# Hybrid decoder step: the prompt tiles' output projection, norm, modulation and routers move between the sample batches

## The chip, the cores and the metric

One core of a Trainium2 chip runs the kernel. Its engines work side by side, each through its own program in order: TensorE (PE, matrix products and transposes), VectorE (DVE), ScalarE (ACT), GpSimd (POOL) and SyncE (SP, which here only sends for transfers). Semaphores tie them together. The metric is the device time of one execution in microseconds; less is better.

## The reference, cut to what matters

One layer is computed for two groups of tokens with the same weights: a prompt of 256 tokens (two tiles of 128 rows), and 8 samples of 8 new tokens (one tile of 64 rows), each sample with a cache of 2048 keys and values. All is float32, D = 1024.

```
shift1, scale1, gate1, shift2, scale2, gate2 = split(silu(c) @ w_ada + b_ada)   # per sequence
u   = x * (1 + scale1) + shift1
q, k, v, B, C, h = split(u @ w_in)
mix = concat(rms(attention(q, k, v, cache)), rms(B * conv3(C * h))) @ w_o
x   = LN1(alpha * x + (1 + gate1) * mix)
u2  = x * (1 + scale2) + shift2
x   = LN2(alpha * x + (1 + gate2) * MoE(u2))    # router, top 4 of 32 experts, clamped SwiGLU
```

gate1, shift2 and scale2 are one vector of 1024 for the prompt and one for each of the 8 samples. The outputs are both groups' x, the new keys, values and convolution rows.

## The kernel before, in words

The stages follow one another on PE, whose program is written out by hand; the other engines' programs mirror it.

1. *Start*: w_ada and w_in stream through a ring of six buffers; PE computes the modulation vectors (kept as 32-row groups in `ada_sb`, bias added), and all projections of all 320 tokens (`q_t`, `k_t`, `v_nat`).
2. *Prompt attention*, head by head, and the turning of the first sample's keys. Then the table of position biases (`s_bias`), and the norm of the prompt's attention output: `squares(0)`, `sums_of_squares(0)`, `mean_squares(0)`, a root on ACT, then `inverse_roots(0)` and `scale(0)`, which run on DVE in batch 7.
3. *Sample batches*, one for each of 8 samples (`pe_batch`, `dve_batch`, `act_batch`; batches 1 to 6 are a hardware loop). PE: scores against 1280 cached keys and the 64 new ones (line 1368), `heads_apart` of the batch before (L1376), transposes of the next batch's keys (`keys(0)`, `keys(1)`, through `turn`, L1155), transposes of the probabilities (L1155), `keys(2)`, product with V (L1417). ACT and DVE copy the turned keys out of PSUM in turns (L558, L819); DVE adds the bias and takes the maximum (L936 to L941), ACT the exponential (L601); DVE takes the reciprocal (L956) and makes the masked output (L961). K and V have one buffer each: SP sends for the next K once the keys are turned, and for the next V when the product with V has used it.
4. *The stage behind the batches*. PE: `output(0)`, `sums_of_squares(1)`, `output(1)` (L1445), `output(2)` (L1438), and three routers (transposes of u2, L1155; 8 products with the router's weights, L1462; the bias, L1463). DVE, in an order written out: residual(0), residual(1), route(0), residual(2), route(1), route(2). `residual` is the gated residual, the layer norm (`layer_norm`, L1720 to L1727) and the modulation (L1002, L1003); `route` (L1010 to L1024) picks four experts and makes the gates. gate1, scale2 and shift2 come as rows of 128 or 64 partitions: POOL wrote them to DRAM during the prompt's attention, and SP reads them back with a broadcast (`mod_p`, `mod_s`). Then the ranks of tokens in each expert (L1480, L1484) and the first gather (L1495).
5. *Experts*: a loop over 32 experts (the data asks for no second round), in which PE uses each expert's 12 MB of weights as they land, then the last norm.

PSUM has 8 banks of 512 columns. In a batch the scores lie in banks 0 to 2, turned keys in 3 to 6, turned probabilities in 5 to 7, the product with V in 7.

## Time and profile before

| | |
|---|---|
| median of 3 runs | 1557.39 us (1557.28 to 1561.96) |
| the profiled execution's own time | 1561.42 us |
| its span, first to last instruction | 1559.6 us |
| mean granted clock of PE | 0.962 of full speed |
| busy: PE, DVE, ACT | 1439.7, 496.6, 244.1 us |
| read from DRAM | 519.87 MB, 336 GB/s over the span |

The span is 2 us short of the same execution's time, and that execution was 4 us longer than the median. Times of single instructions come from this one execution. PE's busy time is that of its products with modelled ends; every float32 product shows as two records. The granted clock is given as a share of 2.4 GHz: 0.50 is the lower of two levels, 1.2 GHz. A wait is written behind an instruction as [idle before it <- what ended the idle time]; "issue" means that the profile shows nothing that was waited for.

### The profile page before, as it was taken

What the parts mean: (1) busy time and instruction counts of PE and PEld (TensorE: products, weight loads), DVE (VectorE), ACT (ScalarE), POOL (GpSimd) and SP (SyncE); (2) the same over time, 40 slices, a digit from 0 to 9 for tenths busy, and PEclk for the clock granted to TensorE, in tenths of its full rate; (3) what the DMA queues carried; (4) which work ended last, traced back from release to release, by engine and by line L of the source; (5) the groups of instructions that cost most, each with busy time, mean ns of one, the idle gap of its engine ahead of it and who ended that gap; (6) DMA issues with size and microseconds to landing.
All of it is one profiled execution on the core that took longest, in us unless ns stands there. A gap on an engine that the chain in (4) does not pass through costs nothing.

```text
span 1559.6 us, 22176 instructions
## 1 busy us (share of the span) xinstructions
PE 1439.7 (92%) x7709; PEld 595.4 (38%) x7710; DVE 496.6 (32%) x1129; ACT 244.1 (16%) x431; POOL 12.0 (1%) x20
## 2 busy tenths in 40 slices
PE   5999998898967999999999999999999999999993
PEld 1654655655442333333333333333333333333331
DVE  2111354444382222322232212232232232222236
ACT  0001423332020111111111101111111111111110
POOL 0000000000010000000000000000000000000000
PEclk9999999999877999999999999999999999999997
DMA  9958268996663679999999988999999999988940
GB/s 341 364 209 319 103 254 315 365 347 261 206 257 128 252 324 387 410 416 417 418 417 415 418 341 324 380 417 417 418 417 416 418 418 416 417 348 317 387 203 34
DMA packets 95700, 523.72 MB, mean 336 GB/s; under 512 B 10156, under 2 KB 10469, under 8 KB 55482
## 3 DMA queue, kind: packets, MB, share of 16 engines
q1 hardware_dynamic: 92496, 517.62, 83.5%
q0 software_dynamic: 1344, 4.90, 0.8%
q10 hardware_dynamic: 1834, 0.84, 0.2%
q8 instruction: 17, 0.28, 0.1%
q14 instruction: 9, 0.07, 0.0%
HBM read 519.87 MB, written 3.46 MB: 336 GB/s over the span
## 4 chain that ended last, share of the span: by engine, by line
PE 86%; DVE 5%; issue 3%; DMA 2%; ACT 2%; SPq 0%; DVEq 0%; ACTq 0%
PE ps L1573 29%; PE ps L1649 15%; PE ps L1517 7%; PE ps L1155 7%; PE ps L1495 5%; PE ps L1215 5%; PE ps L1417 3%; PE ps L1368 2%; PE ps L1565 2%; PE ps L1212 2%; PE ps L1445 2%; DMA arena<-in_w_ada 2%; PE ps L1583 1%; PE ps L1190 1%; ACT arena L672 1%
## 5 line engine op out<-in xcount | busy, mean ns | idle before, releaser
L1573 PE MATMUL ps<-arena 128*64 128x512 f32 x2048 | 460.1, 607 | 0.5 <-issue 0.5
L1573 PEld LDWEIGHTS ps<-arena 128*64 128x64 f32 x2048 | 146.4, 139 | 312.5 <-issue 312.5
L1649 PE MATMUL ps<-arena 128*64 128x512 f32 x1024 | 228.5, 599 | 20.5 <-ACT arena L672 15.1
L1155 PE MATMUL ps<-arena 128*128 128x128 f32 (+4 forms) x1075 | 153.7, 283 | 46.5 <-DVE arena L819 12.5
L1058 DVE TENSOR_TENSOR arena<-arena,ps 128x512 f32<-128x512 f32 (+1 forms) x198 | 123.9, 680 | 203.4 <-PE ps L1517 197.9
L1155 PEld LDWEIGHTS ps<-arena 128*128 128x128 f32 (+4 forms) x1075 | 116.7, 144 | 120.8 <-issue 77.2
L1102 DVE TENSOR_SCALAR arena<-ps 128x512 f32<-128x512 f32 (+1 forms) x35 | 24.2, 692 | 426.7 <-PE ps L1573 360.5
L1649 PEld LDWEIGHTS ps<-arena 128*64 128x64 f32 x1024 | 73.5, 137 | 155.0 <-issue 155.0
L1517 PE MATMUL ps<-arena 64*128 64x512 f32 x444 | 114.6, 622 | 2.2 <-ACT arena L655 2.0
L1495 PE MATMUL ps<-arena 128*64 128x512 f32 (+1 forms) x396 | 98.5, 613 | 2.6 <-DVE arena L1046 2.6
L666 ACT ACTIVATE arena<-arena 128x512 f32<-128x512 f32 (+1 forms) x35 | 22.1, 632 | 456.8 <-DVE arena L1102 456.8
L1215 PE MATMUL ps<-arena 128*128 128x320 f32 x288 | 83.9, 444 | 3.1 <-DVE arena L749 3.1
L1517 PEld LDWEIGHTS ps<-arena 64*128 64x128 f32 x444 | 36.6, 185 | 76.6 <-issue 59.7
L1215 PEld LDWEIGHTS ps<-arena 128*128 128x128 f32 x288 | 54.9, 195 | 28.4 <-issue 5.6
L1082 DVE COPY arena<-ps 128x512 f32<-128x512 f32 (+1 forms) x37 | 24.2, 664 | 108.9 <-PE ps L1155 108.9
L704 ACT COPY arena<-ps 128x512 f32<-128x512 f32 x29 | 17.0, 587 | 258.4 <-PE ps L1517 258.4
L1495 PEld LDWEIGHTS ps<-arena 128*64 128x64 f32 (+1 forms) x396 | 25.5, 137 | 69.3 <-issue 69.3
L666 ACT ACT_TABLE_LOAD x32 | 41.1, 1283 | 38.0 <-issue 38.0
L558 ACT COPY arena<-ps 128x512 f32<-128x512 f32 (+1 forms) x63 | 32.3, 513 | 91.5 <-PE ps L1155 91.5
L1417 PE MATMUL ps<-arena 128*32 128x256 f32 (+1 forms) x528 | 42.7, 395 | 2.2 <-DMA arena<-in_cache_v 2.2
L1368 PE MATMUL ps<-arena 128*32 128x512 f32 (+2 forms) x384 | 39.5, 462 | 2.2 <-DVE arena L923 2.2
L819 DVE COPY arena<-ps 128x512 f32<-128x512 f32 (+1 forms) x63 | 37.2, 599 | 12.8 <-PE ps L1155 11.8
(225 smaller groups left out, 862.0 us busy)
## 6 DMA issues: line engine op xcount, KB each, us to landing
arena<-in_w_up SPq DMA_DIRECT2D x256, 1024.0 KB, 12.8
arena<-in_w_down SPq DMA_DIRECT2D x128, 1024.0 KB, 10.8
arena<-in_w_ada SPq DMA_DIRECT2D x12, 2048.0 KB, 17.5
arena<-in_cache_k SPq DMA_DIRECT2D x16, 1536.0 KB, 8.7
arena<-in_cache_v SPq DMA_DIRECT2D x16, 1536.0 KB, 9.0
arena<-in_w_in SPq DMA_DIRECT2D x6, 2048.0 KB, 20.4
arena<-in_cache_k SPq DMA_DIRECT2D x32, 192.0 KB, 4.1
arena<-in_cache_v SPq DMA_DIRECT2D x32, 192.0 KB, 9.6
```

The source lines that it names most:

```text
L558: nc.scalar.copy(kt_sb[:, c, 512 * kt:512 * kt + w], bank(key_bank(kt * AC + c), 0, w)).then_inc(kt_act, 1)
L666: nc.scalar.activation(act_s[0:p, v, :], act_g[0:p, v, :], ACT.Sigmoid, scale=1.702).then_inc(sig_ready[v], 1)
L819: v_.tensor_copy(kt_sb[:, c, 512 * kt:512 * kt + w], bank(key_bank(kt * AC + c), 0, w)).then_inc(kt_dve, 1)
L1058: ins = v_.tensor_tensor(acc[0:n, tt, 512 * h:512 * h + 512], acc[0:n, tt, 512 * h:512 * h + 512], bank(banks[h])[0:n], ALU.add)
L1155: return nc.tensor.transpose(o, i, ident[0:n, 0:n])
L1215: ins = mm(bank(unit_bank(u))[:, 0:NTOK], w[:, k, col:col + 128], u_t[:, k, :], start=k == 0, stop=k == KC - 1)
L1368: ins = mm(o[32 * j:32 * j + 32], qbd[:, c, :], rhs(c), start=c % 2 == 0, stop=c % 2 == 1, tile_position=(0, 32 * j))
L1417: ins = mm(bank(7, 0, 256)[32 * g:32 * g + 32], pt_sb[0:n, j, 32 * g:32 * g + 32], rhs, start=j == 0, stop=j == KB, tile_position=(0, 32 * g))
L1495: ins = mm(bank(4)[64 * h:64 * h + 64], sel[0:n, tt, 0:MAIN], u2[0:n, tt, 512 * h:512 * h + 512], start=tt == 0, stop=tt == 2)
L1517: ins = mm(bank(banks[h]), sel_t[64 * h:64 * h + 64, v, 128 * tt:128 * tt + 128], y_sb[64 * h:64 * h + 64, v, :], start=v == 0, stop=v == ...
L1573: ins = mm(bank(part)[64 * h:64 * h + 64], xe_t[:, 0, at:at + 64], up_w[:, k, FF * part + 512 * h:FF * part + 512 * h + 512], start=False, ...
L1649: ins = mm(bank(3)[64 * h:64 * h + 64], a_t[:, 0, at:at + 64], dn_w[:, kk, 512 * h:512 * h + 512], start=kk == 0, stop=kk == KC - 1)
```

## The change

- Memory: the batches' buffers (`s_bias`, `prob`, `pt_sb`, `qbd`, `o_mask`) move from R1 and R2 into R4, over the prompt's q, k and v, which are now kept apart from the samples' (`q_p`, `q_s`, `k_p`, `k_s`, `v_p`, `v_s`). R1 and R2 are then free during the batches for `x1` and `u2`.
- x and the gains and offsets of LN1 are loaded by POOL's queue during the batches, not by SP's behind them. The write of the modulation vectors to DRAM and their broadcast back are gone.
- The rows of gate1, scale2 and shift2 are made by PE: a product of a matrix of zeros and ones (`rep_p`, `rep_s`) with the 32-row group of `ada_sb`, two products of 512 columns for a vector.
- `inverse_roots(0)` and `scale(0)` run in batch 0. `output(0)` and `output(1)` run in batches 1 and 2, into banks 0 and 1, from which ACT copies them to `u2`. The prompt's modulation products run in batches 3, 5 and 6; DVE does the residual and the statistics of both tiles in batch 3, the norm in 4, the scale in 5 and the shift in 6. ACT takes the norm's roots in batch 4. In batch 7 PE makes the samples' three vectors (ACT copies them to `mod_s`) and runs the routers of tiles 0 and 1.
- Behind the batches only the samples' norm, `output(2)`, residual(2), router(2) and route(2) are left in front of the ranks.
- The loop over the batches is written out on all three engines.

```diff
-        mod_p = view(W + 18 * D, 3, D)
-        mod_s = view(W + 21 * D, 3, D)
+        mod_s = view(W + 18 * D, 3, D)
...
+        v_s = view(R4, DA)
+        v_p = view(R4 + 768, 2, DA)
+        v_tile = [v_p[:, 0], v_p[:, 1], v_s]
+        q_p = view(R4 + 2304, AC, SEQ)
+        q_s = view(R4 + 3840, AC, 64)
+        k_p = view(R4 + 4224, AC, SEQ)
+        k_s = view(R4 + 5760, AC, 64)
+
+        s_bias = view(R4 + 768, SB)
+        prob = view(R4 + 768 + SB, NCACHE + 64)
+        pt_sb = view(R4 + 4224, KB + 1, 96)
+        qbd = view(R4 + 4224 + (KB + 1) * 96, AC, 32)
+        o_mask = view(R4 + 4224 + (KB + 1) * 96 + AC * 32, 256)
...
-            sp.wait_ge(so_copied, NB)
-            sp.dma_start(x1[:, 0:2, :], t["x_prompt"][0].rearrange("(a p) d -> p a d", p=128)).then_inc(tail_in, 16)
-            for a, name in enumerate(("ln1_g", "ln1_b")):
-                sp.dma_start(ln1[:, a, :], t[name][0:1, :].to_broadcast([128, D])).then_inc(tail_in, 16)
-            sp.wait_ge(vec_out, 64)
-            sp.dma_start(mod_p, vectors[0:1, 0:3 * D].to_broadcast([128, 3 * D]).rearrange("p (a b) -> p a b", a=3)
-                         ).then_inc(mod_in, 16)
-            for b in range(NB):
-                src = vectors[1 + b:2 + b, 0:3 * D].to_broadcast([NS, 3 * D]).rearrange("p (a b) -> p a b", a=3)
-                sp.dma_start(mod_s[NS * b:NS * b + NS], src).then_inc(mod_late, 16)
-            sp.dma_start(x1[0:64, 2, :], t["x_sample"].rearrange("b s d -> (b s) d")).then_inc(mod_late, 16)
...
-            pool.wait_ge(ada_late, 1)
-            for j in range(4):
-                pool.dma_start(vectors.rearrange("r (m j c) -> j r m c", m=2, j=4)[j],
-                               ada_sb[32 * j:32 * j + 1 + NB, 1:3, :]).then_inc(vec_out, 16)
             pool.wait_ge(out_kv, 96)
+            pool.wait_ge(sb_done, 1)
+            pool.dma_start(x1[:, 0:2, :], t["x_prompt"][0].rearrange("(a p) d -> p a d", p=128)).then_inc(tail_in, 16)
+            pool.dma_start(x1[0:64, 2, :], t["x_sample"].rearrange("b s d -> (b s) d")).then_inc(tail_in, 16)
+            pool.dma_start(ln1[1], t["ln1_b"][0:1, :].to_broadcast([128, D])).then_inc(tail_in, 16)
+            pool.wait_ge(og_ready, 1)
+            pool.dma_start(ln1[0], t["ln1_g"][0:1, :].to_broadcast([128, D])).then_inc(tail_in, 16)
...
-                    ins = nc.scalar.mul(q_t[:, c, :], src[:, 0:NTOK], HD ** -0.5)
+                    nc.scalar.mul(q_p[:, c, :], src[:, 0:SEQ], HD ** -0.5)
+                    ins = nc.scalar.mul(q_s[:, c, :], src[:, SEQ:NTOK], HD ** -0.5)
...
+            def act_mix(tt):
+                act.wait_ge(wo_done, tt + 1)
+                for h in range(2):
+                    ins = nc.scalar.copy(u2[:, tt, 512 * h:512 * h + 512], bank(h))
+                ins.then_inc(mix_ready, 1)
+
+            def act_keep_mods(a):
+                act.wait_ge(mods_done, a + 1)
+                for h in range(2):
+                    ins = nc.scalar.copy(mod_s[0:64, a, 512 * h:512 * h + 512], bank(3 + h)[0:64])
+                ins.then_inc(mods_kept, 1)
...
+                if b == 4:
+                    act.wait_ge(var_ready, 2)
+                    nc.scalar.activation(st[:, 66:68], st[:, 64:66], ACT.Sqrt).then_inc(sd_ready, 1)
...
+                if b in (1, 2):
+                    act_mix(b - 1)
...
+            for b in range(NB):
+                act_batch(b)
+            for a in range(3):
+                act_keep_mods(a)
+            act_turn(0)
+            act_exp(0)
+            act_turn(1)
+            act_exp(1)
...
+            def prompt_residual():
+
+                dve.wait_ge(mod_done, 1)
+                for tt in range(2):
+                    V(v_.scalar_tensor_tensor(u2[:, tt, :], ps[:, 0:D], 1.0, u2[:, tt, :], ALU.add, ALU.mult))
+                dve.sem_inc(mod_used, 1)
+                dve.wait_ge(tail_in, 64)
+                for tt in range(2):
+                    V(v_.scalar_tensor_tensor(x1[:, tt, :], x1[:, tt, :], ALPHA, u2[:, tt, :], ALU.mult, ALU.add))
                     for h in range(2):
-                        ins = v_.scalar_tensor_tensor(m[:, 512 * h:512 * h + 512], mod[0:n, 0, 512 * h:512 * h + 512], 1.0,
-                                                      bank(4)[64 * h:64 * h + 64], ALU.add, ALU.mult)
+                        ins = v_.bn_stats(st[:, 48 + 6 * h:54 + 6 * h], x1[:, tt, 512 * h:512 * h + 512])
                     V(ins)
-                dve.wait_ge(tail_in, 48)
-                x_t = x1[0:n, tt, :]
-                V(v_.scalar_tensor_tensor(x_t, x_t, ALPHA, m, ALU.mult, ALU.add))
-                layer_norm(dve, V, v_, x_t, n, st, ln1, var_ready, sd_ready, tt + 3, x_t)
-                V(v_.scalar_tensor_tensor(u2[0:n, tt, :], mod[0:n, 2, :], 1.0, x_t, ALU.add, ALU.mult))
-                V(v_.tensor_tensor(u2[0:n, tt, :], u2[0:n, tt, :], mod[0:n, 1, :], ALU.add))
-                dve.sem_inc(u2_ready, 1)
+                    V(v_.bn_aggr(st[:, 60 + 10 * tt:62 + 10 * tt], st[:, 48:60]))
+                    V(v_.tensor_scalar(st[:, 64 + tt:65 + tt], st[:, 61 + 10 * tt:62 + 10 * tt], LN_EPS, None, ALU.add))
+                dve.sem_inc(var_ready, 1)
+
+            def prompt_normal():
+
+                dve.wait_ge(sd_ready, 2)
+                V(v_.reciprocal(st[:, 66:68], st[:, 66:68]))
+                for tt in range(2):
+                    x_t = x1[:, tt, :]
+                    V(v_.scalar_tensor_tensor(x_t, x_t, st[:, 60 + 10 * tt:61 + 10 * tt], ln1[0], ALU.subtract, ALU.mult))
+                    V(v_.scalar_tensor_tensor(x_t, x_t, st[:, 66 + tt:67 + tt], ln1[1], ALU.mult, ALU.add))
+
+            def prompt_scaled():
+
+                dve.wait_ge(mod_done, 2)
+                for tt in range(2):
+                    V(v_.scalar_tensor_tensor(u2[:, tt, :], ps[:, 0:D], 1.0, x1[:, tt, :], ALU.add, ALU.mult))
+                dve.sem_inc(mod_used, 1)
+
+            def prompt_shifted():
+
+                dve.wait_ge(mod_done, 3)
+                for tt in range(2):
+                    V(v_.tensor_tensor(u2[:, tt, :], u2[:, tt, :], ps[:, 0:D], ALU.add))
+                    dve.sem_inc(u2_ready, 1)
+                dve.sem_inc(mod_used, 1)
...
+                if b == 0:
+                    inverse_roots(0)
+                    scale(0)
+                if b == 3:
+                    prompt_residual()
+                if b == 4:
+                    prompt_normal()
+                if b == 5:
+                    prompt_scaled()
+                if b == 6:
+                    prompt_shifted()
+                if b == 7:
+                    route(0)
+                    route(1)
...
+            residual(2)
+            route(2)
...
+            GATE1, SHIFT2, SCALE2 = (1, 0), (1, 2), (2, 0)
+
+            def modulation(which, n, lhs, b, done):
+
+                m, j = which
+                for h in range(2):
+                    at = 32 * (j + h)
+                    ins = mm(bank(b + h)[0:n], lhs[at:at + 32, 0:n], ada_sb[at:at + 32, m, :], start=True, stop=True)
+                ins.then_inc(done, 1)
+
+            def beside_batch(b):
+                if b == 1:
+                    pe.wait_ge(og_ready, 1)
+                    pe.wait_ge(wo_in, 16)
+                if b in (1, 2):
+                    output(b - 1)
+                if b in (3, 5, 6):
+                    if b == 3:
+                        pe.wait_ge(ada_late, 1)
+                    modulation({3: GATE1, 5: SCALE2, 6: SHIFT2}[b], 128, rep_p, 0, mod_done)
+                if b == 7:
+                    for a, which in enumerate((GATE1, SCALE2, SHIFT2)):
+                        if a:
+                            pe.wait_ge(mods_kept, a)
+                        modulation(which, 64, rep_s, 3, mods_done)
+                    router(0)
+                    router(1)
+
+            def banks_free(b):
+
+                if b in (2, 3):
+                    pe.wait_ge(mix_ready, b - 1)
+                if b in (4, 6, 7):
+                    pe.wait_ge(mod_used, {4: 1, 6: 2, 7: 3}[b])
...
+                if more:
+                    beside_batch(b)
...
+                if not more:
+                    beside_batch(b)
+                pe.wait_ge(v_in, b * 96 + 96)
...
+            for b in range(NB):
+                pe_batch(b)
+            heads_apart(NB - 1)
+
+
+            pe.wait_ge(so_copied, NB)
             sums_of_squares(1)
-            output(1)
             pe.wait_ge(og_ready, 2)
             output(2)
-            router(0)
-            router(1)
             router(2)
```

## Rows read from the trace of the kernel before

**Rows 1.** The page's chain that ended last: shares of the span by engine.

```profile
PE 86%; DVE 5%; issue 3%; DMA 2%; ACT 2%; SPq 0%; DVEq 0%; ACTq 0%
```

**Rows 2.** Windows: stretch, its length, busy time (instructions), granted clock, DMA share, GB/s.

```profile
243.87:265.77 21.90, 19.45 (x200) 12.97 (x203) 9.50 (x24) 7.77 (x13) 0.00 (x0) 1.00 0.93 345
...
403.00:441.00 38.00, 37.92 (x112) 16.59 (x112) 17.06 (x31) 1.80 (x3) 0.00 (x0) 0.96 0.97 320
...
446.00:456.20 10.20, 6.13 (x26) 5.55 (x26) 9.48 (x27) 2.78 (x4) 0.00 (x0) 0.50 0.43 145
```

**Rows 3.** Order of time, TensorE, a middle batch: start, duration, instructions [idle before].

```profile
328.89 1.54 PE L1155 MATMUL ps<-arena 96*128 96x96 f32 x15 [0.77 <-ACT arena L558]
...
332.69 5.08 PE L1417 MATMUL ps<-arena 128*32 128x256 f32 x66
```

**Rows 4.** Order of time, DVE and ACT, the same middle batch and the next scores.

```profile
323.39 1.42 ACT L601 ACTIVATE arena<-arena 96x1344 f32<-96x1344 f32 x1
...
333.03 0.16 DVE L956 RECIPROCAL arena<-arena 96x1 f32<-96x1 f32 x1
...
342.61 0.22 DVE L936 SCALAR_TENSOR_TENSOR arena<-ps,arena 96x64 f32<-96x64 f32 x1 [4.24 <-PE ps L1368]
```

**Rows 5.** Order of time, batch 7, all engines and SP's transfers of V.

```profile
381.06 0.81 SPq L372 DMA_DIRECT2D arena<-in_cache_v  x2
...
382.09 3.34 DVE L872 RECIPROCAL arena<-arena 128x512 f32<-128x512 f32 x1
...
390.16 2.00 PE L1155 MATMUL ps<-arena 96*128 96x96 f32 x11 [2.50 <-ACT arena L601]
...
392.60 0.24 DVE L952 COPY arena<-ps 64x96 f32<-64x96 f32 x1
...
392.95 2.47 DVE L877 SCALAR_TENSOR_TENSOR arena<-arena 128x256 f32<-128x256 f32 x6
...
394.32 6.35 PE L1417 MATMUL ps<-arena 128*32 128x256 f32 x66 [2.17 <-DMA arena<-in_cache_v]
```

**Rows 6.** Order of time, TensorE, from batch 7 to the first expert.

```profile
403.08 15.70 PE L1445 MATMUL ps<-arena 128*128 128x512 f32 x32 [0.30 <-DVE arena L929]
...
420.34 13.95 PE L1445 MATMUL ps<-arena 128*128 128x512 f32 x32
434.23 7.09 PE L1438 MATMUL ps<-arena 128*64 128x512 f32 x32
...
449.38 1.94 PE L1155 MATMUL ps<-arena 128*128 128x128 f32 x8 [3.63 <-DVE arena L1012]
...
455.55 0.63 PE L1463 MATMUL ps<-arena 1*128 1x32 f32 x2
...
470.00 2.41 PE L1480 MATMUL ps<-arena 128*128 128x32 f32 x12 [3.41 <-DVEq L1028]
...
489.13 1.13 PE L1565 MATMUL ps<-arena 1*64 1x512 f32 x4 [3.04 <-issue]
```

**Rows 7.** Order of time, DVE and ACT, the same stretch.

```profile
420.98 1.28 ACT L594 ACT_TABLE_LOAD   x1 [29.19 <-DVE arena L867]
...
425.18 1.22 DVE L990 SCALAR_TENSOR_TENSOR arena<-arena,ps 128x1024 f32<-128x1024 f32 x1
...
429.26 0.15 DVE L1723 TENSOR_SCALAR arena<-arena 128x1 f32<-128x1 f32 x1
...
451.94 1.39 DVE L995 SCALAR_TENSOR_TENSOR arena<-arena,ps 64x512 f32<-64x512 f32 x2
...
460.65 1.22 DVE L1003 TENSOR_TENSOR arena<-arena 64x1024 f32<-64x1024 f32 x1
...
466.69 0.18 DVE L1010 COPY arena<-ps 64x32 f32<-64x32 f32 x1 [1.39 <-PE ps L1463]
```

**Rows 8.** The product of line 1527: duration ns min/median/max, first and last start, forms.

```profile
L1527 PE MATMUL ps<-arena x12: 585/587/692, 1526.4 to 1533.7; 32*128 32x512 f32 x8, 32*64 32x512 f32 x4
```

More of the change, by code:

```diff
@@ new lines, in _, with residual @@
+            queries(slice(0, NS))
+            for b in range(NB):
+                dve_batch(b)
+            keep_output(NB - 1)
+            dve.wait_ge(so_copied, NB)
+            dve.wait_ge(po_copied, AC)
+            dve.wait_ge(out_kv, 96)
+            squares(1)
+            mean_squares(1)
+            inverse_roots(1)
+            scale(1)
+            def residual(tt):
+                n = TILES[tt][1]
+                m = mix[0:n]
+                dve.wait_ge(mods_kept, 3)
+                dve.wait_ge(wo_done, tt + 1)
+                for h in range(2):
+                    ins = v_.scalar_tensor_tensor(m[:, 512 * h:512 * h + 512], mod_s[0:n, 0, 512 * h:512 * h + 512], 1.0,
+                                                  bank(4)[64 * h:64 * h + 64], ALU.add, ALU.mult)
+                V(ins)
+                x_t = x1[0:n, tt, :]
+                V(v_.scalar_tensor_tensor(x_t, x_t, ALPHA, m, ALU.mult, ALU.add))
+                layer_norm(dve, V, v_, x_t, n, st, ln1, var_ready, sd_ready, tt + 2, x_t)
+                V(v_.scalar_tensor_tensor(u2[0:n, tt, :], mod_s[0:n, 1, :], 1.0, x_t, ALU.add, ALU.mult))
+                V(v_.tensor_tensor(u2[0:n, tt, :], u2[0:n, tt, :], mod_s[0:n, 2, :], ALU.add))
+                dve.sem_inc(u2_ready, 1)
@@ L1449, in router @@
             def router(tt):
-                n = TILES[tt][1]
+                n, first = TILES[tt][1], 0 if tt < 2 else 6
                 pe.wait_ge(u2_ready, tt + 1)
@@ L1461, in router @@
                 for k in range(KC):
[L1462 to L1467 removed]
+                    mm(bank(first, 0, NE)[0:n], u2_t[tt][:, k, 0:n], rw_sb[:, k, :], start=k == 0, stop=False)
+                mm(bank(first, 0, NE)[0:n], ones[0:1, 0:n], rb_sb[0:1, :], start=False, stop=True).then_inc(lg_done, 1)
```

283 lines of the change are left out of this document (122 added, 161 removed).

## The prediction

> **What bounds the kernel now.** I read the page's chain first. TensorE has 86% of it, DVE 5%, DMA 2% [rows 1]: this is a kernel in which the order on one engine sets the time, and a microsecond put on that engine is lost unless it fills a hole there. Then I read the table of windows [rows 2]. A middle sample batch takes 21.90 us, of which PE is busy 19.45; the DMA engines are busy 93% of it too, so either could be the pace. The order of time of a batch decides it [rows 3]: PE's holes are three or four of 0.3 to 0.8 us, each ended by a copy out of PSUM on DVE or ACT (0.77 before the transposes of the probabilities), and V's product starts with no wait for a transfer. In eight batches one transfer is waited for, V of batch 7, for 2.17 us [rows 5]. So batches are paced by PE and have about 2.4 us of holes each, made of short hand-overs that stay where they are.
>
> Behind the batches lies the stage that the change takes apart. From the end of V's product in batch 7 (394.32 + 6.35 = 400.7) to the first expert's bias product at 489.13 [rows 5, 6] there are 88.5 us. Its first half is the three output products, PE busy 37.92 of 38.00 us [rows 2]; behind them DVE works already on tile 0. Its second half, from 441 on, is a chain of short steps through DVE, ACT and PE at a granted clock of 0.50 [rows 2, 6, 7]. The experts behind it are the same program in both versions, and start later or earlier as a whole. So the account has two columns: what each batch grows by, and what is left of the 88.5 us.
>
> **The change, part by part.** *Output products of tiles 0 and 1*, 16 products of 512 columns each, go between batches 1 and 2, in front of the transposes and behind the waits for exp and the key copies, so they fill none of the holes. They took 15.70 and 13.95 us in the stage [rows 6]; the first began at a lower clock. In the batches the clock is 1.00 [rows 2], so 13.95 each: **+27.9**. Their results are copied by ACT (two of 512 columns) ahead of its last key copies; those wait in part anyway: 0 to 1.2 us a batch, I take **+0.5** in all.
>
> *Modulation rows by products.* Two products each with 32 rows contracted. The same form stands at the end of the kernel: 4 records of 585 ns, that overlap [rows 8], at 0.43 start to start 1.7 us per vector. Three vectors for the prompt, in batches 3, 5 and 6: **+5.2**. In exchange the writes to DRAM and the broadcast reads go; they lay on queues under the output products and nobody waited for them: 0.
>
> *Work on DVE in the batches.* It is put behind the reciprocal of a batch and ahead of the masked output. Between these the engine has, from 333.03 to the next scores at 342.61, 9.6 us, less 0.5 for the masked output itself [rows 4]. Batch 0 gets the inverse roots and the scaling: 3.34 + 2.47 and two more of the same form, 0.9, is 6.7 us [rows 5]. Batch 3 gets the residual and the statistics of two tiles: one tile took 425.18 to 429.41, 4.2 us [rows 7], two 8.5. Batch 4 gets 5.3 us, 5 and 6 get 2.5 each (steps of 1.2 to 1.3 us). All fit under V's product and the next scores, batch 3 with 0.6 us to spare: 0. With that cover gone, the next scores' maximum would be late by as much, and PE behind it.
>
> *A square root among the exponentials.* ACT's table changes in front of batch 0's exp, and in batches 4 and 5. A load is 1.28 us [rows 7]. Behind the exp of a batch (1.42 us) stand the key copies that free PE's banks [rows 4], so in batch 4 load and root, 1.5 us, come through; batch 5's load stands between a copy and the exp, 1.3; batch 0's 0.7. From nothing to 4: **+3.5**. The Trainium skill (ScalarE: Activation LUTs, "What ACT_TABLE_LOAD costs" and "Table sets") speaks against this edit: each switch is 1.283 us of load and about 1.38 of drain, and all calls of one set should be made before the next. The load agrees with the row; no drain shows in the transition's record, where the root starts as the load ends. By the page's sum three switches would cost 4.1 us more.
>
> *Batch 7.* Once PE has turned the probabilities and they are copied (392.60 + 0.24, [rows 5]) it does, in front of V's product, the sample's three modulation vectors, each waiting for two ACT copies of the one before, and then two routers, the second waiting for DVE's maximum of the first. V came in at 394.3, so only 1.3 us of this lies in a hole. A router at the half clock ran from 449.38 to 456.2, 6.8 us; 6.2 of them are PE's own, so at full clock some 4 to 4.5 [rows 6]. The vectors: three of 1.7 and two gaps of 1.4 are 7.9 us, at half clock 13.0. With 0.75 between the routers the block is 17.5 us at full clock and 27.3 at half. PE had been at half clock when it came here (its transposes took 2.00 us for 11 records, against 1.54 for 15 in a middle batch [rows 3, 5]), and the stretch of the second router in the trace stayed at 0.50 throughout, with PE busy 6.13 of 10.20 us [rows 2]. So I take it near the half-clock end: 25.3, less the 1.3: **+24** (bounds 16 and 26).
>
> *What is left of the stage*, counted from the end of V's product: masked output, heads apart, copy, as before, 2.4 (403.08 less 400.7); squares 0.9 (estimate, by columns from the 1.22 us of 1024); sums of squares 1.6 (between the two output products); mean to scaled, 420.34 to 425.2, 4.9; output of tile 2 7.09, and 1.75 for a clock that fell in this gap, as at 403; residual of tile 2, 451.94 to 461.9, 10.0; router 462.9 to 466.7, 3.9; routing 466.69 to 470.00, 3.3; from there to 489.13 unchanged, 19.1 [rows 6, 7]. Sum 55.1 against 88.5: **-33.4** (bounds -35 without the clock, -28 if tile 2's whole product ran at half). Note what goes: 29.65 of it is the two products, which are paid again in the batches; the rest of the old chain is shorter by about 11, but the norm of the sample tokens, which hid under tile 1's product, lies bare now, 7.4 us.
>
> *Free or nearly so.* The first expert's weights wait, as before, for the last use of V; 8 MB at the 3.93 MB in 13 us that V takes [rows 5] are 27 us, and 55 us hold them. The q and k copies split in two lie under projections of 4 us. Inputs x and the norm's vectors come early by another queue, 2.25 MB, in batches 0 and 1, which have got longer.
>
> Sum: 27.9 + 0.5 + 5.2 + 3.5 + 24 - 33.4 = **+27.7 us**. The profiled execution's own time was 1561.4 (span 1559.6), so 1589 for one like it. The median of the runs shown is 4.0 below it: **1585 us**.
>
> **Rivals.** *1. The transfers pace the batches.* If DMA at 93% were the limit, the 33 us of inserted PE work would vanish in it, and -33.4 + 24 + 4 leaves 1552: faster. It tips the sign if more than 27.7 of the 33.1 is hidden. For it: the share. Against: no batch but the last waits for a transfer; V is sent for at 381.06 and is there at 394.3, 13 us, where a middle batch has 16.8 from one use to the next (21.90 less 5.1, [rows 2, 3]). 0.05. *2. The clock stays high in batch 7*, and the table switches hide: 16 in place of 24 and 1 for 3.5, 1574. 0.15. *3. DVE is the new wait*: its 8.5 us in batch 3, or the seven pieces with their semaphores, overrun, 1 to 2 us in four batches, and tile 2's product runs at half clock: some +8, 1593. 0.13. *4. The chain is sped up by less waiting than I count* (hand-overs of PSUM while PE is on output products close holes of 2.4 us in six batches and the routers overlap): at most -14 from holes, 1571; it would need the full clock too to come near 1557. 0.03, with a third of it no change. The forecast itself 0.64, its own range 1577 to 1592.
>
> **How the numbers follow.** All low bounds together give 27.9 + 0 + 5.2 + 0.7 + 16.2 - 35.1 = +15, 1572; all high ones 27.9 + 2.4 + 5.2 + 4.1 + 26 - 28 = +38, 1595. The range reaches a little past both: 1570 to 1596; rival 1 and what is unthought of stay outside. A measurement here tells 0.3%, 4.7 us, from no change. Faster: rival 1, 0.05. Same: 0.02. Slower: 0.93.
>
> **What would show it.** Batches 1 and 2 of about 36 us, with PE never waiting for a transfer; 3, 5, 6 about 23.6; in batch 7 some 25 us between the transposes' copies and V's product, at a granted clock near 0.5; some 55 us from there to the first expert's bias product; experts at their old period. I am wrong if batches 1 and 2 are under 30 us (then transfers were the pace), if batch 7's block is under 15, or if the last stretch is under 45.

## The result and the profile after

The changed kernel takes **1586.02 us** (median of 4 runs, 1583.29 to 1590.64) against 1557.34 of the kernel before on the same chip: ratio 1.0176 (95%: 1.015 to 1.0202). It is slower, by 28.7 us; forecast were 1585.0 and a range of 1570 to 1596. A second comparison gave 1587.77 against 1558.03, ratio 1.0202 (1.0181 to 1.0222). The profiled execution of the changed kernel took 1583.29 us, its span is 1581.1. One of the four executions of the doubled products below took 6975 us, in a slow state, and is left out there.

The page's slices and chain of the kernel after:

```profile
PE   4999989988774999999999999999999999999994
...
PEclk9999999999765999999999999999999999999997
...
PE 86%; DVE 6%; issue 3%; ACT 3%; DMA 2%; SPq 0%; DVEq 0%; ACTq 0%
```

and the same two slices of the kernel before:

```profile
PE   5999998898967999999999999999999999999993
...
PEclk9999999999877999999999999999999999999997
```

The chain is still TensorE's [rows 1]. The dip in the 11th to 13th slices (395 to 514 us in the kernel after) has become longer and deeper: PE's busy share is 7, 7 and 4 tenths where it was 9, 6 and 7, and its clock 7, 6 and 5 where it was 8, 7 and 7. Three windows of the kernel after (stretch, length, busy time and instructions of PE, its weight loads, DVE, ACT, POOL, granted clock, DMA share, GB/s): a batch with an output product in it, the new block of batch 7, and the last stretch ahead of the experts.

```profile
277.02:312.52 35.50, 33.28 (x232) 19.01 (x235) 9.46 (x24) 7.34 (x14) 0.00 (x0) 1.00 0.60 223
422.90:445.90 23.00, 18.04 (x64) 12.00 (x64) 3.28 (x21) 5.83 (x11) 0.00 (x0) 0.50 0.00 1
490.00:512.00 22.00, 14.71 (x63) 6.87 (x63) 8.63 (x50) 2.56 (x4) 0.00 (x0) 0.50 0.30 119
```

A middle batch of before was 21.90 us with 19.45 of PE [rows 2]; with the output product it is 35.50 with 33.28: 13.6 us more, for 13.8 more of PE, so next to nothing was filled. DMA's share fell from 0.93 to 0.60 and the batch is longer by the whole product, so transfers were not the pace. In batch 7 PE's clock is 0.50, with PE busy 18.04 of 23.00 us.

TensorE in order of time, kernel after, batches 1 to 6 (start, duration, instructions, idle before and what ended it):

```profile
259.37 13.97 PE L1463 MATMUL ps<-arena 128*128 128x512 f32 x32 [0.98 <-ACT arena L557]
...
276.95 5.08 PE L1561 MATMUL ps<-arena 128*32 128x256 f32 x66
...
312.45 5.08 PE L1561 MATMUL ps<-arena 128*32 128x256 f32 x66
...
330.48 1.13 PE L1490 MATMUL ps<-arena 32*128 32x512 f32 x4 [0.88 <-ACT arena L557]
331.54 1.57 PE L1223 MATMUL ps<-arena 96*128 96x96 f32 x15
...
351.75 2.40 PE L1223 MATMUL ps<-arena 128*128 128x128 f32 x20 [1.42 <-ACT arena L557]
...
376.06 2.40 PE L1223 MATMUL ps<-arena 128*128 128x128 f32 x20 [1.09 <-ACT arena L557]
```

L1463 is the output product of a prompt tile in two halves of 512 columns, L1561 the product with V, L1490 a modulation vector. The starts of V's product in batches 0 to 6 are 241.23, 276.95, 312.45, 335.36, 359.27, 384.11 and 406.90: batches of 35.7, 35.5, 22.9, 23.9, 24.8 and 22.8 us where they had been 21.9 (two of them 22.4 and 22.7 in the profiled execution). The modulation costs 1.06 us a batch (330.48 to 331.54), not 1.7. The last two lines are new waits of batches 4 and 5, behind the table loads on ACT. PE waits for no transfer between 241 and 446.

The same view from batch 7 to the first expert:

```profile
406.90 5.08 PE L1561 MATMUL ps<-arena 128*32 128x256 f32 x66
...
423.33 1.97 PE L1490 MATMUL ps<-arena 32*64 32x512 f32 x4 [0.84 <-DVE arena L1039]
426.45 1.97 PE L1490 MATMUL ps<-arena 32*64 32x512 f32 x4 [1.15 <-ACT arena L624]
429.58 1.97 PE L1490 MATMUL ps<-arena 32*64 32x512 f32 x4 [1.16 <-ACT arena L624]
431.48 1.97 PE L1223 MATMUL ps<-arena 128*128 128x128 f32 x8
...
439.17 1.94 PE L1223 MATMUL ps<-arena 128*128 128x128 f32 x8 [0.87 <-DVE arena L1004]
...
445.90 6.84 PE L1561 MATMUL ps<-arena 128*32 128x256 f32 x66
...
456.10 2.57 PE L1414 MATMUL ps<-arena 128*128 128x64 f32 x12 [1.19 <-DVE arena L886]
...
464.34 9.88 PE L1456 MATMUL ps<-arena 128*64 128x512 f32 x32 [4.81 <-DVE arena L905]
484.39 1.11 PE L1223 MATMUL ps<-arena 64*128 64x64 f32 x8 [10.17 <-DVEq L1092]
...
491.57 2.41 PE L1582 MATMUL ps<-arena 128*128 128x32 f32 x12 [3.34 <-DVEq L1096]
...
512.27 1.99 PE L1667 MATMUL ps<-arena 1*64 1x512 f32 x8 [2.38 <-issue]
```

From 423.33 to 445.90 lies the new block: 8.15 us of modulation (three vectors of 1.97, the end of each included, and two gaps) and 14.4 us of two routers. Behind V's product, which ends at 452.7, come the sums of squares (L1414), the norm (a hole of 4.81), the output product of tile 2 (L1456, 9.88 against 7.09 in [rows 6]), its residual (10.17 of PE's idle time), the last router and the routing. The first expert's bias product is at 512.27, against 489.13 [rows 6].

The account of the two profiled executions:

| stretch | before | after | difference | forecast |
|---|---|---|---|---|
| to V's product of batch 0 | 243.79 | 241.23 | -2.6 | +0.7 |
| V's product of batch 0 to that of batch 6 | 132.70 | 165.67 | +33.0 | +36.4 |
| V's product of batch 6 to that of batch 7 | 17.83 | 39.00 | +21.2 | +24 |
| from there to the first expert's bias | 94.8 | 66.4 | -28.4 | -33.4 |
| to the first expert | 489.13 | 512.27 | **+23.1** | **+27.7** |

Of the first difference 1.7 us are not the change's: batch 0's scores took 6.42 us at a lower clock in the execution before and 4.72 in this one, and in the second profile of the changed kernel they took 6.42 again. The sum is 4.6 us short of the forecast, and the medians are nevertheless 28.7 and 29.7 apart.

One part of what is missing lies in the experts, which I had taken as unchanged. From one expert's bias product to the next, an ordinary expert takes 29.86 us before and 30.08 after, in all of the 22 ordinary gaps: 22 x 0.22 = 4.8 us. Two more gaps went from 33.13 to 33.33. The other seven, the first and six around experts with two blocks, differ from execution to execution (38.4 to 42.1 the first; 44.2 or 45.9 and 32.5 or 34.1 the six), and in the profiled pair they fell to the advantage of the changed kernel by 7 us: the experts' whole stage (first to last bias product) took 1005.0 us before and 1003.0 after. That is why the spans differ by 21.5 us only. A second profile of each kernel gives the same picture: first bias 489.51 and 513.57, periods 29.86 and 30.08, stage 1005.3 and 1003.1. Both profiles of the kernel before were 4 us above its median and both of the changed kernel 3 us below its own. That 23.1 + 4.8 = 27.9 is near the medians' distance is thus a reckoning which takes the seven gaps as equal in the long run; no profile shows a pair that far apart.

### The profile page after: what moved, and what is told of

The parts are those of the page before. It is cut to its first block, busy times and chain, and to the rows that moved or that the text cites. A ratio compares the mean times of both kernels' runs of the same rounds, so it can differ in the third digit from the quotient of the medians.

```text
span 1581.1 us, 21918 instructions
## 1 busy us (share of the span) xinstructions
PE 1446.4 (91%) x7733; PEld 627.1 (40%) x7734; DVE 496.5 (31%) x1134; ACT 241.3 (15%) x440; POOL 12.1 (1%) x20
## 4 chain that ended last, share of the span: by engine, by line
PE 86%; DVE 6%; issue 3%; ACT 3%; DMA 2%; SPq 0%; DVEq 0%; ACTq 0%
PE ps L1675 28%; PE ps L1751 14%; PE ps L1619 7%; PE ps L1223 7%; PE ps L1597 5%; PE ps L1283 5%; PE ps L1561 2%; PE ps L1667 2%; DMA arena<-in_w_in 2%; PE ps L1437 2%; PE ps L1280 2%; PE ps L1463 2%; PE ps L1685 1%; ACT arena L696 1%; PE ps L1258 1%
## 5 line engine op out<-in xcount | busy, mean ns | idle before, releaser
L1675 PE MATMUL ps<-arena 128*64 128x512 f32 x2048 | 453.0, 599 | 0.0
L1675 PEld LDWEIGHTS ps<-arena 128*64 128x64 f32 x2048 | 148.8, 138 | 302.6 <-issue 302.5
L1751 PE MATMUL ps<-arena 128*64 128x512 f32 x1024 | 228.3, 597 | 26.6 <-ACT arena L696 20.5
L1751 PEld LDWEIGHTS ps<-arena 128*64 128x64 f32 x1024 | 97.0, 137 | 137.4 <-issue 135.0
L1561 PE MATMUL ps<-arena 128*32 128x256 f32 (+1 forms) x528 | 43.1, 398 | 0.0
L1667 PE MATMUL ps<-arena 1*64 1x512 f32 x256 | 35.7, 627 | 4.9 <-issue 4.5
```

The costliest lines, as they stand in the source:

```text
L1561: ins = mm(bank(7, 0, 256)[32 * g:32 * g + 32], pt_sb[0:n, j, 32 * g:32 * g + 32], rhs, start=j == 0, stop=j == KB, tile_position=(0, 32 * g))
L1667: ins = mm(bank(part)[64 * h:64 * h + 64], ones[64 * part:64 * part + 1, 0:64], row, start=True, stop=False)
L1675: ins = mm(bank(part)[64 * h:64 * h + 64], xe_t[:, 0, at:at + 64], up_w[:, k, FF * part + 512 * h:FF * part + 512 * h + 512], start=False, ...
L1751: ins = mm(bank(3)[64 * h:64 * h + 64], a_t[:, 0, at:at + 64], dn_w[:, kk, 512 * h:512 * h + 512], start=kk == 0, stop=kk == KC - 1)
```

## The experiments

All were compared with the kernel before on the same chip (its medians: 1558.03 for the first four, 1559.01 for the next two, 1559.09 for the three paddings, 1558.88 for the last two). "First bias" is the start of the first expert's bias product in the profile.

### What the two kernels scatter by

The kernels before and after, unchanged, with more runs.

> The kernel before, once more with a profile, since the one profiled execution was 4 us above the median of its kernel and that of the changed kernel 3 us below its own. Theory A (the difference lies between 225 and 490 us: 23 us in the two profiles, and the rest is which execution was profiled): the time to the first expert's bias product is again 489 us within 2, the experts' period 29.87, and the execution's scatter of 4 us lies in the experts' stage or in the first transfers. Rival B (the experts' period is itself a property of each program): the period is 29.87 in every execution of this kernel and 30.08 in every one of the changed kernel.

> The changed kernel once more with a profile. Theory A: first bias product at 512 us within 2, ratio of the medians 1.015 to 1.018, and the experts' period is 29.87 or 30.08 by chance of the execution. Rival B: the period is 30.08 again, some 0.21 us for each of 25 ordinary experts, 5 us of the difference, which my sum does not have at all and which comes from something in the program other than the moved work.

Measured: before 1558.24 (10 runs), ratio 1.0002 (0.9987 to 1.0018), first bias 489.51; after 1587.77, ratio 1.0202, first bias 513.57. The ratio of the changed kernel was expected at 1.015 to 1.018 and came out above; the two comparisons of it lie 0.3% apart. The period is 29.86 in both profiles of the kernel before and 30.08 in both of the changed one, so it belongs to the program and not to an execution.

### Are the output products hidden in the batches?

The products of batches 1 and 2 are made twice, into the same banks; the work is the reference's, done twice.

```
                 if b in (1, 2):
+                    output(b - 1, False)    # no semaphore at its end
                     output(b - 1)
```

> The products of output(0) and output(1) in batches 1 and 2 are made twice over; nothing else changes. Theory A (batches are paced by TensorE, and what is put in adds its whole length): batches 1 and 2 grow from 35.7 to 49.6 us each and the kernel by 27.9 us. Rival (transfers set the pace, products in the batches are partly hidden): they grow by less than 10 each, and the kernel by under 20.

Measured: 1603.52 (the three executions of 1602 to 1607 us), ratio 1.0306 (1.0282 to 1.0329), first bias 538.34. TensorE in order of time:

```profile
262.73 27.70 PE L1463 MATMUL ps<-arena 128*128 128x512 f32 x64 [0.98 <-ACT arena L557]
...
311.96 27.70 PE L1463 MATMUL ps<-arena 128*128 128x512 f32 x64 [0.77 <-ACT arena L557]
```

The two batches take 49.4 and 49.2 us, 13.7 longer each: a microsecond put here is a microsecond lost, up to twice the amount that the change put in, and the wait ahead of the product is the same 0.98 and 0.77. This ends rival 1. But the kernel became slower by 16 to 17 us only, not by 27.9; by the kernel's time alone the rival ("under 20") would have won, and it is the length of the two batches that decides. The first bias came 24.8 to 26.1 us later, and the experts behind it were faster: 997.2 us from first to last bias product for 1003.0, with a period of 29.87 us. This miss made me follow the experts' period, below.

### The square root among the exponentials

ACT's root for batch 4 moved behind its last key copies of batch 3.

```
-                if b == 4:
+                if b == 3:       # now behind act_turned(2, b + 1)
                     act.wait_ge(var_ready, 2)
                     nc.scalar.activation(st[:, 66:68], st[:, 64:66], ACT.Sqrt)...
```

> The root of the prompt's norm moves from behind the exp of batch 4 to the end of batch 3 on ScalarE, where that engine is idle; the number of table loads stays. Theory A (the load and root in front of batch 4's key copies cost PE 1.3 us there, and the load in front of the exp a further 1.1 in the next batch): batch 4 loses the wait of 1.42 us behind ACT but gets the one of 1.09 in front of its exp, batch 5 loses its 1.09; the kernel is 1.2 to 1.6 us faster. Rival (the hand-overs take it up elsewhere): no difference.

Measured: 1585.44, ratio 1.0184 (1.0166 to 1.0202), first bias 510.40. The waits of batches 4 and 5:

```profile
355.01 2.40 PE L1223 MATMUL ps<-arena 128*128 128x128 f32 x20 [1.32 <-ACT arena L557]
...
375.41 3.71 PE L1223 MATMUL ps<-arena 128*128 128x128 f32 x32 [0.47 <-DVE arena L844]
```

The wait of batch 5 is gone; that of batch 4 stays, because a table load now stands ahead of its exp. From V's product of batch 4 to that of batch 5 are 22.8 us (361.97 to 384.78) in place of the 24.1 of the second profile of the changed kernel (361.18 to 385.29). The first bias is 1.9 to 3.2 us earlier than in the two profiles of the changed kernel; the medians' difference, 2.3 us, lies within the intervals. In these two batches a change of table costs PE 1.1 to 1.3 us of waiting, about the 1.28 of a load, and by this edit only one of the two can be put where ACT has time.

### The routers of tiles 0 and 1 out of batch 7

Router 0 stands behind the sample tokens' sums of squares, its routing on DVE under tile 2's output product; router 1 behind that product; tile 1's transposed tile gets a place of its own. ACT's and DVE's steps follow PE's new order: on ACT the root of the sample tokens' norm goes ahead of the routers' copies and exponentials, on DVE the two routings go behind the norm and behind tile 2's residual.

```
-                    router(0)               # at batch 7, ahead of V's product
-                    router(1)
...
             sums_of_squares(1)
+            router(0)
             pe.wait_ge(og_ready, 2)
             output(2)
+            router(1)
             router(2)
```

> The routers of tiles 0 and 1 leave batch 7. Router 0 stands behind the samples' sums of squares, where TensorE waits 4.8 us for the norm; route(0) on DVE runs under the output product of tile 2; router 1 stands behind that product and route(1) behind the residual of tile 2. Theory A (they were in front of V's product with nothing beside them, 14.4 us in series): batch 7 shrinks from 39.0 us to 24.6, the stage behind it grows by 2 to 4 us, the kernel is 10 to 12 us faster than the changed one, 1574 us or so, still slower than before by 15 to 18. Rival (the time in front of V's product was partly V's own transfer or would be waited for anyway): under 6 us faster.

Measured: 1570.99, ratio 1.0075 (1.0055 to 1.0095), first bias 499.11. TensorE in order of time (line numbers 2 to 4 lower than in the changed kernel):

```profile
433.48 6.58 PE L1557 MATMUL ps<-arena 128*32 128x256 f32 x66
...
446.86 1.91 PE L1221 MATMUL ps<-arena 128*128 128x128 f32 x8
...
454.28 8.44 PE L1454 MATMUL ps<-arena 128*64 128x512 f32 x32
...
473.70 1.09 PE L1221 MATMUL ps<-arena 64*128 64x64 f32 x8 [6.88 <-DVE arena L1003]
...
499.11 1.98 PE L1665 MATMUL ps<-arena 1*64 1x512 f32 x8 [3.05 <-issue]
```

V's product starts at 433.48 in place of 445.90, right behind the last modulation. Router 0 fills the hole in which DVE and ACT do the norm (4.81 us before tile 2's product above; now none), and router 1, which starts on PE at 462.65, part of the 10.17 us of tile 2's residual, of which 6.88 are left. From the end of V's product (440.06) to the first bias are 59.0 us, against 59.5 without any router of tiles 0 and 1 in it: they cost nothing there, where they cost 14.4 in batch 7. The first bias comes 13.2 to 14.5 us earlier and the median is 15 to 17 lower, both more than the 10 to 12 expected: I had reckoned with a part that stays bare. So about half of what the change costs is the place of two routers: in front of V's product, with holes behind it that nothing filled. The ordinary period of this kernel is 30.08, so the gain doesn't lie in the experts.

### A wait of the kernel before

In the kernel before, DVE waits once for the root of tile 1's norm, because ACT does tile 0's transposed copies first.

```
-            for step, tt in ((act_root, 0), (act_turn, 0), (act_root, 1), (act_exp, 0), ...
+            for step, tt in ((act_root, 0), (act_root, 1), (act_turn, 0), (act_exp, 0), ...
```

> The kernel before with one order changed on ScalarE: the root for tile 1's norm stands ahead of the copies of tile 0's turned u2. In the profile of before DVE waited 3.65 us for that root, since ScalarE first waited for router 0's transposes. Theory A (the stretch from 441 to 470 us is a chain through DVE): 3.3 us faster than before, 1554 us. Rival (the routers on TensorE, or their copies, then end last): under 1 us.

Measured: 1556.49 (12 runs), ratio 0.9972 (0.9957 to 0.9988), first bias 485.26. DVE in order of time, the reciprocal in the kernel before and then the same place in this one:

```profile
443.14 0.16 DVE L1725 RECIPROCAL arena<-arena 128x1 f32<-128x1 f32 x1 [3.65 <-ACT arena L623]
```

```profile
438.96 0.15 DVE L1723 TENSOR_SCALAR arena<-arena 128x1 f32<-128x1 f32 x1
439.38 0.16 DVE L1725 RECIPROCAL arena<-arena 128x1 f32<-128x1 f32 x1 [0.27 <-ACT arena L623]
```

The wait was 3.65 us and is 0.27. The first bias comes 3.9 to 4.3 us earlier. The medians are 2.5 us apart and the ratio says 4.4, with an interval from 2 to 7. Part of what the changed layout removes from the stage was thus to be had in the old one by a swap.

### Why do the experts take 0.22 us more each?

The doubled products had brought the old period back, with nothing changed in the experts: what they did change was that PE's program ahead of its loop was longer. So I put small transposes of 8 rows, each overwritten by the next, near the start of PE's program.

```
+            for _ in range(64):             # or 32
+                turn(bank(6, 64, 72), g_rows[0:8, :], 8)
```

> The changed kernel with 64 more transposes of an 8-row tile at the start of TensorE's program, where it waits for x and w_ada anyway: 128 more instructions in front of everything, as many as the doubled products had. In the runs so far the period of an ordinary expert was 29.86 in the kernel before and with the doubled products, and 30.08 in four others, with the same instructions in the loop. Theory C (the period follows from where TensorE's loop lies in its program, not from what runs in it): it goes to 29.87, the experts' stage is about 6 us shorter and the kernel 4 to 6 us faster than the changed one, with the first bias product where it was. Rival (the doubled products' time between the batches did it, through the transfers or the clock): the period stays 30.08 and the time is that of the changed kernel.

> The same with 32 transposes, 64 instructions. Theory C: the period is 29.87 or 30.08 according to the place, which I cannot foresee for this one; any other value or a period that moves within the run speaks against it. The time to the first bias product stays within 2 us of the changed kernel's.

> The kernel before with the 64 transposes at its start. Theory C: its period may go from 29.86 to 30.08, and the kernel would then be 4 to 6 us slower, with nothing else changed; if it stays at 29.86, the two kernels differ in which places are good, and the time stays at 1558. Rival (the changed kernel's loop is slower for another reason, its buffers or its data): the period is 29.86.

Measured:

| kernel | median us | ratio (95%) | first bias | ordinary period |
|---|---|---|---|---|
| after, 64 more | 1578.46 | 1.0135 (1.0115 to 1.0155) | 513.37 | 29.86 |
| after, 32 more | 1577.84 | 1.0142 (1.0115 to 1.0169) | 517.07 | 29.86 |
| before, 64 more | 1553.31 | 0.9973 (0.996 to 0.9987) | 484.26 | 29.86 |

More instructions make the changed kernel 7.6 to 9.9 us faster by the medians, and its first bias is not earlier. The period is worth 4.8 of that. The rest I can't place, and no profile shows it: the profiled executions took 1581.56 us with 64 and 1588.49 with 32, both above their medians, and their experts' stages were 1000.2 and 1003.7 us long for 1003.0 without padding, since the gaps around two blocks took their longer values. With 32, four executions took 1577.1 to 1578.0 us and two 1588.5 and 1589.3, and one of the two was profiled. Its first bias, 517.07, is outside the 2 us expected; 3.2 us of that are a longer wait just ahead of it (5.61 for 2.39; the profile shows nothing that was waited for).

One ordinary expert of the kernel after, its down product (L1751), TensorE in order of time:

```profile
681.28 1.09 PE L1223 MATMUL ps<-arena 128*128 128x128 f32 x8
683.18 7.09 PE L1751 MATMUL ps<-arena 128*64 128x512 f32 x32 [0.80 <-ACT arena L696]
```

and TensorE's weight loads in the same place:

```profile
682.95 0.42 PEld L1751 LDWEIGHTS ps<-arena 128*64 128x64 f32 x4 [0.81 <-issue]
```

The same two views of the kernel with 64 more transposes (L1753 is the same line), matmuls and then weight loads:

```profile
681.20 7.09 PE L1753 MATMUL ps<-arena 128*64 128x512 f32 x32 [0.58 <-ACT arena L696]
```

and

```profile
681.20 0.20 PEld L1753 LDWEIGHTS ps<-arena 128*64 128x64 f32 x4 [0.81 <-issue]
```

The four loads stand over 0.42 us in place of 0.20, and PE starts 0.2 us later in each of the 22 ordinary gaps (0.18 to 0.22): that is the whole difference in period. One by one the loads are no longer than before, 0.13 us each. The first of them starts 0.58 us behind the transposes, as in the kernel before (682.95 behind 682.37); the second and the first product start 0.23 us behind it (683.18), where they had started together with it. So the time passes between the first load and the instruction after it. It is shown that adding instructions ahead of PE's loop, 64 or 128 at the start or 128 in the batches, restores 29.86, that the changed kernel, root_early and routers_late, without them, have 30.08, and that the work in the loop is the same. Whether the cause is where the loop's instructions lie, and in which unit, was not settled; no row shows how they are fetched.

In the kernel before, whose period was right already, the 64 transposes still gave 4 to 6 us; it was expected to stay at 1558. Its profiled execution is the fastest of its 12 (1548.63), and there the difference from the first profile of the kernel before can be placed. At the first bias it is 4.9 us (484.26 for 489.13): 1.7 in batch 0's scores (4.72 for 6.42), 1.3 in batches 3 and 4, the rest behind. In the experts it is 8.0 (997.0 for 1005.0): 2.8 in the first gap and 1.7 in each of three around two blocks. The granted clock goes with it: 0.92 in the first gap for 0.88, 1.00 in the third for 0.95. What the transposes have to do with the clock in these places was not followed.

### The better of each

The changed kernel with the routers late, the root early and 64 transposes; and the kernel before with its root first and 64 transposes.

> The changed kernel with all three: routers 0 and 1 behind the batches, the root at the end of batch 3, the 64 transposes at the start. If the three are independent, 1587.8 less 17, 2 and 9 is 1560 us, level with before; the first bias product at 497 to 499 us, 8 to 10 later than before. If the place of the loop turns out badly for this program (its period would be 30.08), 1566.

> The kernel before with the root of tile 1 first and the 64 transposes at its start. They gave -2.5 and -5 us alone. Independent: 1551 us, first bias product 481 to 486 us, faster than both kernels. If the transposes' gain in before was the clock's phase only and not the program's, it may not add: 1555.

Measured: changed 1562.97 (11 runs), ratio 1.004 (1.0026 to 1.0054), first bias 497.88, period 29.86; before 1548.86 (10 runs), ratio 0.9948 (0.9933 to 0.9963), first bias 484.09. The second beats both kernels: it is 10 us below the kernel before and 37 below the changed one's 1586.02. At the first bias its two edits don't add (484.09 with both, 485.26 and 484.26 alone); the other 8 us against the first profile of before lie in the experts' stage, 996.9 for 1005.0, as with the transposes alone. The mended change remains 14 us behind the mended kernel before, which is the distance of the first biases, 13.8; the experts' stages are 996.7 and 996.9. What is left lies wholly ahead of the experts.

## Why the prediction came out

The time was right to 1 us, and the mechanism held ahead of the experts: two output products paid in full in the batches, the routers bare in batch 7, and a stage that gave back less than that. The nearness is partly luck: the path to the experts was overestimated by 3.6 to 4.6 us, and the experts, which had no step of their own in the sum, account for 4.8 us by their period; where the rest of the medians' distance lies is not shown.

- **Bound.** That a microsecond put on PE in a batch is lost held to 0.2 us: the two batches are 13.8 and 13.6 us longer for a product of 13.8, and 13.7 more each when doubled. Rival 1 (transfers) is refuted by this. Of the holes that rival 4 wanted closed, PE's wait ahead of the second key transposes went from 0.66 to 0.47 us, and the others stayed.
- **Output products**: forecast +27.9, measured 27.6. **ACT's copies**: 0.5 forecast, the waits grew by no more than 0.1 to 0.2.
- **Modulation rows**: +5.2 was mis-sized; measured 3 x 1.06 = 3.2. I had priced a vector by the wrong row. [rows 8] is the product of line 1527, the experts' down biases, and both its halves lie on the same 32 rows (`gt_sb[0:NE]`): three of their 4 records start 0.43 us behind the one before, and the next product starts after 1.91. The two products of a vector lie on different groups of 32 rows, as those of line 1535 (`gate2`) do. That line stands next to the other in the same profile, at clock 1.00 too, and has the 1.13 us of the vectors in the batches:

```profile
1523.98 1.13 PE L1535 MATMUL ps<-arena 32*128 32x512 f32 x4
...
1526.38 1.98 PE L1527 MATMUL ps<-arena 32*128 32x512 f32 x4
```

By that row the forecast would have been about +3.2 to 3.4. The Trainium skill (TensorEngine Tiling (Array Packing), "Key Properties") says that tiles of the array work independently and can load and multiply in parallel; the 1.13 on two groups of rows, for two products that take 1.98 on one, agrees with it.
- **Root and table**: forecast +3.5. The waits of batches 4 and 5 are 2.3 us longer than in other batches together, and batch 0's change of table costs PE 0.1 (from its scores to V's product 16.68 us, against 16.58 in the kernel before with 64 transposes, whose scores also took 4.72). The term is 2.4. In this execution PE's clock was also 0.78 from 357 to 365, which makes the transposes and V's product there 1.3 us longer; that is not the root's, for both profiles of the kernel before have the same 1.3 us in batches 3 and 4 and the second of the changed kernel does not. I had also overlooked that the kernel before loads a table in every batch from 0 to 6, where ACT is idle behind V's start (244.29 and so on); the change doesn't add loads, it puts two of them where PE waits. The Trainium skill (ScalarE: Activation LUTs, "What ACT_TABLE_LOAD costs") would have added a drain of about 1.38 us to each switch; the trace doesn't agree, as it shows none: the exp's last record ends at 349.70, the load of 1.28 us starts at 349.72, and the root at 351.02.

```profile
349.72 1.28 ACT L636 ACT_TABLE_LOAD   x1
351.02 0.21 ACT L636 ACTIVATE arena<-arena 128x2 f32<-128x2 f32 x1
```

- **DVE in batch 3**: costed at 0 with 0.6 us to spare. It is 8.8 us and just fits: its last step ends at 344.54, the masked output at 345.19, and the scores that DVE is to take next ended at 345.1. PE's step on it starts 4.87 us after the scores instead of 4.65, so DVE costs 0.2 us here. Rival 3's overrun is refuted, but with nothing to spare; its other half, tile 2's product at the lower clock, came in part (9.88 us, at a granted clock of 0.71). DVE in order of time:

```profile
335.71 0.16 DVE L1043 RECIPROCAL arena<-arena 96x1 f32<-96x1 f32 x1
...
344.71 0.48 DVE L1060 SCALAR_TENSOR_TENSOR arena<-ps,arena 96x256 f32<-96x256 f32 x1 [0.16 <-DVE arena L971]
345.15 0.22 DVE L1023 SCALAR_TENSOR_TENSOR arena<-ps,arena 96x64 f32<-96x64 f32 x1
```

- **Batch 7**: forecast +24, measured +21.2. The clock was at the lower level, as taken (rival 2 refuted). The routers are 14.4 us against 14.3 forecast; the vectors 8.15 against 13.0: the same wrong row as above, doubled for the clock (3.4 a vector, where the view has 1.97), and gaps of 1.15 instead of 1.4. The hole in front of V, taken as 1.3, is 1.5 by [rows 5].
- **The rest of the stage**: -33.4 was mis-sized by 5 us (the steps as listed add up to 54.9, not 55.1). V's product took 6.84 instead of 6.35, and from its end to the first bias it is 59.5 us. The sums of squares took 3.4, not 1.6, tile 2's output product 9.88, not 8.85, and the last stretch, which I had taken from before unchanged (19.1), took 20.7. The granted clock goes with all three: it was 0.66 from V's end to 464.3, 0.71 in tile 2's product, 0.57 behind it and 0.50 in the last stretch, where the same steps had run at 0.68 before. I had given the lower clock one price, 1.75, for the whole path.
- **The experts** "start later or earlier as a whole", "at their old period": this step failed. Their program is the same, but each ordinary one takes 0.22 us longer, 4.8 us in all; in the two profiles of each kernel other gaps, of changing length, outweigh that. With 64 transposes in both, and the same period in both, the two are 1578.46 less 1553.31 = 25.2 us apart; since the transposes also moved the first bias of the kernel before, that is a rough price of the change without this effect, no exact one.

Where the cost lies is shown for half of it by an experiment: the routers' place, 13 to 15 us on the path. The 13.8 us that still part the mended pair are only read from an account of their two profiles, and no run took them apart. Batches 1 and 2 are 27.4 us longer for the output products, and the stage behind the batches only 24.7 shorter, since the chains that these products covered lie bare: 2.7. The modulation vectors make three batches 2.8 longer in sum, and a table load makes batch 4 1.3 longer. Batch 7 is 6.9 longer: the samples' vectors take 8.15, and the wait of 1.69 for V is gone. The change moves two dense products, 29.7 us in the kernel before, out of the one stage that had chains to cover, into batches that had no room for them.

## What to carry to other kernels

Moving dense work off a stage that looks full helps, by this case, only if the place it goes to has holes; look first at what the dense work covers, because the chains under it become bare when it leaves. Put short dependent products (here two routers) behind the product that the next long chain needs, not in front of it. Before pricing a product by a row of the same size, look up in the code whether its operands lie alike: two halves on the same 32 rows cost nearly twice what they cost on different ones. Compare the profiled execution's time with its median before a difference is put down to a stage. When the code ahead of a hot loop changes in length, compare the period of the loop itself before crediting the edit with the difference.

## What the hardware showed that I had not expected

- The same loop of experts takes 29.86 or 30.08 us an iteration, by what stands ahead of it in PE's program: 64 or 32 more small transposes restore the shorter one, and so did the doubled output products. The 0.22 us pass between the first weight load of the down product and the instruction after it. Over 22 experts they are 4.8 us; the medians moved by 7.6 to 9.9.
- With PE busy 18.04 of 23.00 us in steps of 2 to 4 us the granted clock stayed at 0.50 (1.2 GHz), and at 14.71 of 22.00 too; in a batch with 33.28 of 35.50 it was 1.00 (2.4 GHz).
- Two 32-row products of 512 columns take 1.13 us together at clock 1.00 and 1.97 at clock 0.50 when they lie on different groups of 32 rows (L1490 in the kernel after), and 1.98 at clock 1.00 when they lie on the same (L1527 in the kernel before).
- Stretches with the same instructions come in two lengths, 1.7 us apart, from one execution to the next: 44.2 and 45.9, 32.5 and 34.1 for experts around two blocks; 4.72 and 6.42 for batch 0's scores, the longer at a lower clock. The third gap was 32.57 at clock 1.00 in the changed kernel and 34.14 at 0.95 in the kernel before. The experts' stage of one kernel can so differ by 8 us (1005.0 in the kernel before, 997.0 with 64 transposes at its start, both with a period of 29.86).
